# Products that nobody reads, put where TensorE waits, in a two-layer hybrid diffusion step

## What is computed

```python
h = rms_norm(x, norm1_g) * (1 + scale1) + shift1
y = even_mixer(h)      # layer 0: RG-LRU beside differential attention
y = odd_mixer(h)       # layer 1: chunked gated delta rule beside grouped-query attention
x = x + gate1 * y
h = rms_norm(x, norm2_g) * (1 + scale2) + shift2
x = x + gate2 * expert_choice_ffn(h)   # 16 experts, each takes its 80 best tokens
```

## Time and profile before

| what | value |
|---|---|
| median of 3 runs | 1860.54 us (1860.17 to 1864.04) |
| the profiled execution's own time | 1863.33 us |
| its span | 1861.5 us |
| TensorE busy with products and transposes | 1578.3 us, 85% of the span |
| VectorE, ScalarE, GpSimd busy | 647.7, 450.9, 195.5 us |
| mean granted clock of TensorE | 0.922 of full speed |
| DMA | 330.03 MB, mean 177 GB/s |

### The profile page before, as it was taken

The page is one execution under the profiler, slowest core; times in us unless marked ns, Lnnn a source line. Parts: engine busy times, 40 slices in busy tenths (PEclk is TensorE's granted clock), DMA queues, the critical chain, the costliest instruction groups (busy, mean ns, idle before and its releaser), DMA issues.

```text
span 1861.5 us, 37187 instructions
## 1 busy us (share of the span) xinstructions
PE 1578.3 (85%) x16388; PEld 1039.3 (56%) x16388; DVE 647.7 (35%) x1284; ACT 450.9 (24%) x746; POOL 195.5 (11%) x197
## 2 busy tenths in 40 slices
PE   5999965778839999995999977688887957999993
PEld 2554433444517677663555456577775536667762
DVE  5134476552270000004044179734453262000003
ACT  4111284441021111103010055532221031111110
POOL 0000000000001111100000000054640001111103
PEclk8999986998969999997999989788988988999997
DMA  9822370455217999994121100000004225999994
GB/s 342 302 91 90 138 280 6 176 202 205 87 67 274 374 389 383 379 354 136 49 86 49 45 1 1 1 2 3 2 3 159 79 102 175 374 371 391 373 396 153
DMA packets 90316, 330.03 MB, mean 177 GB/s; under 512 B 10709, under 2 KB 16457, under 8 KB 82025
## 3 DMA queue, kind: packets, MB, share of 16 engines
q1 hardware_dynamic: 76016, 287.29, 40.6%
q0 software_dynamic: 9168, 32.65, 6.4%
q10 hardware_dynamic: 5032, 8.65, 1.3%
HBM read 303.79 MB, written 24.78 MB: 177 GB/s over the span
## 4 chain that ended last, share of the span: by engine, by line
PE 72%; DVE 12%; DMA 6%; ACT 5%; issue 5%; POOL 0%; ACTq 0%; DVEq 0%; SPq 0%
PE pairs L192 26%; PE pairs L1245 14%; PE pairs L1257 11%; DMA ring<-in_exp_w 3%; PE pairs L1228 2%; DVE sm L1601 1%; PE pairs L1934 1%; PE pairs L1936 1%; PE pairs L1923 1%; ACT arena L319 1%; PE pairs L961 1%; PE pairs L421 1%; PE pairs L1667 1%; ACT arena L1517 1%; PE pairs L1082 1%
## 5 line engine op out<-in xcount | busy, mean ns | idle before, releaser
L192 PE MATMUL pairs<-hT,ring 128*128 128x128 f32 (+1 forms) x1120 | 305.6, 436 | 2.1 <-ACT hT L319 2.1
L319 ACT ACTIVATE arena<-pairs 128x512 f32<-128x512 f32 (+7 forms) x212 | 129.8, 632 | 501.5 <-PE pairs L192 251.0
L192 PEld LDWEIGHTS pairs<-hT,ring 128*128 128x128 f32 x1120 | 170.2, 192 | 138.3 <-issue 136.8
L192 PE MATMUL pairs<-ring,hT 128*128 128x512 f32 (+1 forms) x448 | 177.4, 557 | 0.0
L1245 PEld LDWEIGHTS pairs<-arena 128*64 128x64 f32 x4096 | 145.5, 139 | 15.1 <-issue 15.0
L1245 PE MATMUL pairs<-arena 128*64 128x80 f32 x4096 | 148.3, 235 | 3.3 <-issue 2.3
L1245 PEld LDWEIGHTS pairs<-arena,ring 128*64 128x64 f32 x4096 | 142.9, 137 | 14.2 <-issue 14.2
L1245 PE MATMUL pairs<-arena,ring 128*64 128x80 f32 x4096 | 145.9, 233 | 0.9 <-issue 0.7
L192 PEld LDWEIGHTS pairs<-ring,hT 128*128 128x128 f32 x448 | 85.0, 190 | 92.0 <-issue 89.0
L1311 DVE TENSOR_SCALAR hT<-pairs,arena 80x512 f32<-80x512 f32 x32 | 23.9, 747 | 274.6 <-ACT hT L1287 274.6
L1257 PE MATMUL pairs<-ring,arena 128*80 128x512 f32 x256 | 112.8, 593 | 1.6 <-DMA ring<-in_exp_w 1.6
(11 more groups left out here) (374 smaller groups left out, 2074.6 us busy)
## 6 DMA issues: line engine op xcount, KB each, us to landing
arena<-in_exp_w SPq DMA_DIRECT2D x48, 2048.0 KB, 19.2
ring<-in_exp_w SPq DMA_DIRECT2D x48, 2048.0 KB, 21.6
ring<-in_w_mod SPq DMA_DIRECT2D x24, 2048.0 KB, 8.0
ring<-in_w_in_ab SPq DMA_DIRECT2D x5, 2048.0 KB, 11.6
ring<-in_w_in_cd SPq DMA_DIRECT2D x5, 2048.0 KB, 8.1
ring<-in_w_out SPq DMA_DIRECT2D x4, 2048.0 KB, 8.0
moe_rows<-arena POOLq DMA_DIRECT2D x2, 2560.0 KB, 15.7
h_rows<-arena POOLq DMA_DIRECT2D x2, 2560.0 KB, 8.4
```

Of the source, the lines that this page charges most:

```text
L192: last = pe.matmul(out, lhs(k), rhs(k), start=(k == 0), stop=(k == KD - 1))
L319: return eng.activation(dst, src, ACT.Copy) if eng is nc.scalar else eng.tensor_copy(dst, src)
```

## The change

A new helper issues n products of the identity with 512 columns of constants, into a PSUM pair or bank that is free at that point; no one reads them, and what is put there next starts its sum anew. The helper is called before the waits named above. In `norm_pe` the pair is also taken ahead of the wait for the squares, and `diff_pe` and `gqa_pe` wait for one unit to be read before the products go to its pair. `spare()` waits for the reader of bank 4's last unit.

```diff
@@ -304,6 +304,11 @@
             pe.wait_ge(S("x_here"), 16 * NT)
             flip_in_pe(pe, "x_in")
 
+        def keep_busy(pe, ps, n):
+
+            for _ in range(n):
+                pe.matmul(ps[:, 0:512], ident, cst[:, 0:4, :].rearrange("p a b -> p (a b)"), start=True, stop=True)
+
         def flip_in_pe(pe, tag):
             for k in range(KD):
                 ps = take(pe, (tag, k))
@@ -479,8 +484,10 @@
 
         def norm_pe(pe, l, n):
             u = ("nrm", l, n)
+            ps = take(pe, u)
+            if n:
+                keep_busy(pe, ps, 2)
             pe.wait_ge(S("sq_add"), ADDS[l, n] + KD - 1)
-            ps = take(pe, u)
             pe.matmul(ps[:, 0:NS], ones, ssum[:, 0:NS], start=True, stop=True)
             finish(pe.matmul(ps[:, NS:T], ones, ssum[:, NS:T], start=True, stop=True), u)
 
@@ -565,6 +572,7 @@
                 ps = take(pe, u)
                 if l == 1 and c == 4 and tp == 0:
 
+                    keep_busy(pe, ps, 6)
                     for k in range(KD):
                         pe.wait_ge(S("h_ready"), 32 * l + 2 * k + 2)
                         for t in range(2):
@@ -946,6 +954,8 @@
                 for t in range(NT):
                     last = pe.transpose(ps[:, t * P:t * P + P], qr[:, t, c], ident)
                 finish(last, u)
+            emptied(pe, ("kT", 2))
+            keep_busy(pe, PSUM[:, units.of["kT", 2][0], :], 3)
             for h in range(4):
                 emptied(pe, ("kT", h))
                 emptied(pe, ("qT", h))
@@ -1258,6 +1269,8 @@
                                              w2[:, f, 512 * half:512 * half + 512], start=(f == 0), stop=(f == FT - 1))
                 last.then_inc(pair_full[3], 1)
 
+            take_at(0, 0, 0)
+            keep_busy(pe, PSUM[:, 0, :], 3)
             gather_T(0, 0)
             beside_first_pe(pe, l)
             base[1:] = units.uses[1:]
@@ -1410,6 +1423,7 @@
         def sum_pe(pe, l):
             un = ("nrm", 1, 0)
             acc = take(pe, un, 3)
+            keep_busy(pe, acc, 12)
             for k in range(KD + 3):
                 if k < KD:
                     if k % 2 == 0:
@@ -1651,6 +1665,8 @@
                 for t in range(NT):
                     last = pe.transpose(ps[:, (t + 1) * P:(t + 2) * P], kdup[:, t, n * P:n * P + P], ident)
                 finish(last, u)
+            emptied(pe, ("gqT", 2))
+            keep_busy(pe, PSUM[:, units.of["gqT", 2][0], :], 3)
             for g in range(4):
                 emptied(pe, ("gqT", g))
             emptied(pe, ("gkT", 0))
@@ -1954,6 +1970,11 @@
                                          vb(j)[r, h, :], start=True, stop=True)
                         if k == 3:
                             b_finish(last, us[h // 2])
+
+            def spare():
+                if banks.uses[4]:
+                    pe.wait_ge(bank_free[4], banks.uses[4])
+                keep_busy(pe, bank_of(4), 1)
 
             def state_a(j):
 
@@ -2000,9 +2021,12 @@
                         if h == 3:
                             b_finish(last, ("st", j, d))
 
+            keep_busy(pe, bank_of(6), 6)
             for m in TILE_ORDER[:2]:
                 kq(m)
+                keep_busy(pe, bank_of(4), 1)
                 kk(m)
+            keep_busy(pe, bank_of(4), 2)
             for j in range(2):
                 am(j)
             for i in range(5):
@@ -2030,13 +2054,17 @@
                     elif s == 5 and i == 2:
                         kk(ST)
                 if i < 4:
-                    for e in range(2):
-                        am(j + 2 + e)
-                for e in range(2):
-                    wu(j + e)
+                    am(j + 2)
+                    spare()
+                    am(j + 3)
+                wu(j)
+                spare()
+                wu(j + 1)
             state_b(8)
             state_a(9)
             state_b(9)
+            pe.wait_ge(bank_free[4], banks.uses[4])
+            keep_busy(pe, bank_of(4), 6)
             pe.wait_ge(S("o_done"), 10)
             for b in range(8):
                 pe.wait_ge(bank_free[b], banks.uses[b])
```

## The result

The changed kernel takes 1834.22 us (median of 4 runs, 1830.64 to 1835.67), the kernel before in the same runs 1862.29 (1860.17 to 1865.01). The ratio is 0.9846, with a 95% interval of 0.9824 to 0.9867: 28 us faster, where 22.5 were forecast. The profiled execution has a span of 1828.7 us and a mean granted clock of 0.954, against 1861.5 and 0.922.

The account below looks back on a forecast made before the run. TensorE was taken to bound the kernel, with gains only from raising its clock behind waits. Terms summed to -24.0 us against 1863.33, giving 1839.3; 1.4 off made 1838 us, range 1828 to 1847 (to 1853 with partial gain and turns).

Parts of the forecast that it names:

- Routers: Norm and router of both layers: products fit the waits, router's low-clock time halves in each layer; -3.2 us.
- first projection: Layer 1's first projection: six products fit a wait of 6.97 us, the 20 passes behind run faster; -2.7 us.
- behind the loop: After the delta rule's loop: six products in a wait of 6.10 us speed the turns behind; -2.1 us.
- Layer 0's experts: Three products in a wait of 5.16 us; turn maybe 0.3 late, first expert faster, whole stage shifts; -2.5 us.
- The sum: Sum between the layers: twelve products end just ahead of the rows; low-clock time behind halves, less later rows; -1.5 us.
- Layer 1's experts: Three products overrun a wait of 1.59 us by 1.0, but the 32 passes behind run faster; -0.9 us.
- Attentions: Differential and grouped-query attention: products overrun their waits by 1.3 and 0.8 us, 1.0 credited back for both; +1.1 us.
- Delta rule: Ahead of the loop: six products in 6.30 us, a bit under half the ceiling of 9; -4 us, ends 0 and 9.
- The ends of rounds: Ends of the delta rule's rounds: spare() holds the clock in short gaps; -8.2 us of 9.7, ends 0 and 9.7.
- the gain reaches the end only in part: Rival, 14%: other engines between TensorE's delta-rule steps limit the gain; about 1849 us.
- Turns hold the clock: Denied by a 3% rival: if turns don't, products ahead of L2053, L1420 and L1877 buy nothing; 1843 us.
- Products that outlast their waits: Slower rival, 6%: clock falls in spite of the products and they outlast their waits; about 1880 us.

Follow-up runs that it names:

- turns: Changed kernel with each product replaced by eight 128x128 transposes; 1834.56 us, ratio 0.9851 to the kernel before.
- Fewer products: Changed kernel without the nine products of the two attentions and of layer 1's experts; 1831.55 us, ratio 0.9833.
- twice as many: Changed kernel with 12 products in place of 6 ahead of both routers and layer 1's first projection; 1842.07 us, ratio 0.9894.
- half as many: Changed kernel without the attentions' and layer 1's experts' products, 3 in place of 6 ahead of both routers and layer 1's first projection; 1837.31 us, ratio 0.9873.
- more fill: Changed kernel with products moved into later attention waits, two more spares in round 3, one product instead of three at layer 1's experts; 1819.93 us, ratio 0.9779.
- The other columns of the table: Distances in two traces: changed kernel with eight transposes for each product (1834.56 us), and with the helper empty (1861.83 us).
- thin spares: Changed kernel with only the nine products of spare() cut to 16 columns; 1845.47 us, ratio 0.9911.
- the second group: Runs of fewer products, twice as many, thin spares and more fill, timed in turn with the kernel before, whose median there was 1862.4 us.

## Why the prediction was right

**The price and the principle.** A product was put at 0.86 us at the high clock; twelve passes took 5.32 with their tail, and six more products cost 3.3 where 5.2 less 1.7 were expected. That the products hold the clock was inferred from other work. It is shown now: the ratio is 0.9995 without them, 0.9967 with 16 columns, 0.9851 with turns, and the nine spares alone lose 11 us when they are cut to 16 columns.

**Routers, first projection, behind the loop.** Forecast -3.2, -2.7 and -2.1, measured -3.2, -2.6 and -1.9. Here the work behind the wait has no gaps, so its time at the low clock could be halved without further thought.

**Layer 0's experts.** Forecast -2.5. The products took 4.76 us, not 5.1, since the clock rose inside them; the turn was not late, and the first expert was over 2.8 us earlier. The stage behind took 1.1 us less in this trace, 0.7 more with turns and 0.4 less without the delta rule's products. No product stands there, so I take it for chance, perhaps of the loads; no run isolates it.

**The sum.** Forecast -1.5, measured -0.8. The row of the step says why, as the prediction had half allowed for: the second quarter of the rows was late.

```profile
845.18 1.31 PE L1434 MATMUL pairs<-cst,arena 128*128 128x128 f32 x10 [0.24 <-DMA arena<-moe_rows]
847.06 1.31 PE L1434 MATMUL pairs<-cst,arena 128*128 128x128 f32 x10 [0.56 <-DMA arena<-moe_rows]
```

At the low clock TensorE had been slow enough never to meet this wait.

**Layer 1's experts.** Forecast -0.9, measured 0: this term was mis-sized. I priced the three products at 0.86 us each, at the high clock. They took 3.34, since the turns ahead of them (L1122) begin behind the long wait for the top-k and run at the low clock, and so did part of the products. Fewer products showed the same time.

**Attentions.** Forecast +1.1, measured -2.0 in this trace and nothing in the medians of the run without them. The overrun is as forecast at the first scores of differential attention (+1.2, for 1.3). What comes back behind them varies by up to 2.7 us from trace to trace, with no product at all. The reason given, that the wait of 3.15 us stays empty, fits: with that wait filled and a product in each later step, the stage gains 5 us on the kernel before, 3.3 of it within the first 16 us.

**Delta rule.** Ahead of the loop the forecast was -4, with ends 0 and 9, and -6.2 came: I took a bit under half the ceiling where two thirds were there. In the changed kernel and eight others with these products the stretch from the first L1877 to the end of round 0's steps takes 34.7 to 34.8 us, all at 1.00, where it took 41.0 at a mean of 0.73, so this is all that the clock had to give there. The ends of rounds were put at -8.2 and brought -9.6, and -12.0 with turns, more than the 9.7 taken for the ceiling, since that left out round 0. Without round 0's 1.6 they brought 8.0 in the changed kernel: round 1's end gave 4.0 where 3.4 was the most expected, round 3's 2.4 of 4.6, round 4's 1.6. So the term came out near its size because what was left out and what was lost about balance.

Round 3's end fell to a mean of 0.73 in this trace, but the empty gap that the prediction named is not enough to bring the clock down. TensorE in order of time ahead of it, and the stretch behind, first the changed kernel:

```profile
1337.65 0.68 PE L1927 MATMUL pairs<-cst,arena 64*64 64x64 f32 x16 [2.34 <-DVE hT L2279]
```

Then the kernel with turns:

```profile
1346.28 0.68 PE L1927 MATMUL pairs<-cst,arena 64*64 64x64 f32 x16 [2.34 <-DVE hT L2279]
1346.30:1355.80 9.50, 8.52 (x146) 1.00 0.02 5
```

The gap is 2.34 us in both, and with turns, with twice as many and with half as many products this end ran at 1.00 and took 9.4 us, where the changed kernel's took 11.8. So it is open what two more spares bring there. With them (more fill) it took 9.4 us too, 2.3 less than in the changed kernel, though the clock fell once ahead of it in that trace, which took 1.5 back.

**The rivals.** That the gain reaches the end only in part was the likeliest of them, and it fell: ahead of the loop a third of the ceiling stayed away though the clock was fully up, but 1834 us is far from its 1849. Turns hold the clock. Products that outlast their waits cost what was said, and but for a part of those at layer 1's experts they ran at the high clock, so no place of the changed kernel lost more than 1.7 us. A penalty under 1% of a typical kernel's span (the Trainium skill, "TensorE: Matmul & The Clock Gate", Part 1) is too small for this kernel: 28 us, 1.5%, came back with the change and 42 us, 2.2%, with the better placed products.

What fell short is the sum: 24.0 forecast, 28.1 measured between the medians, 32.8 between the two spans. Some 5 us of the 32.8 lie where no product was put or none mattered: 1.1 in the rest of layer 0's experts, 1.0 at the decays, 0.6 in the convolution's turns, 2.0 in the attentions. The other columns of the table show the first and the last of these moving in both directions, and the kernel with the delta rule's products alone gained 6.2 us in such places, so I take them for chance. The forecast of 1838 also took 1.4 us off the sum, since the median of three runs lay 2.8 below the profiled execution; the later medians of the kernel before, 1861.3 to 1862.4, lie only 0.9 to 2.0 below it. That the time came within 4 us of the forecast is in part luck: single terms miss by up to 3 us, and they point both ways.

## What to carry to other kernels

Where the engine's clock follows its own work, read each wait together with the clock of the work behind it; half of that work's time at the low level is what can be had, in full where the work has no gaps (in this kernel the routers, the first projection and the turns behind the loop). Fill the wait with work that ends just ahead of the instruction it waits for: in a wait of 6.97 us, 5.2 us of it kept the clock up, 2.6 brought nothing or little at the routers and 1.0 of 2.7 us at the projection, and 10.3 cost 3.3. Where a wait is shorter than the fill, or another empty wait follows it, look for a later place with a free bank before adding anything.

## What the runs showed that I had not expected

- Between an idle stretch and the fall of the clock can lie some work at full speed: with 4.30 us empty the router's first passes took 1.03 us and the second 1.87.
- Near the edge it is chance: the same loop with the same thin spares ran the ends of rounds 0 and 1 at a mean of 1.00 in one kernel and at 0.73 and 0.62 in another, which differ in the products ahead of the loop. Behind the same gap of 2.34 us, and with full spares or turns in it, round 3's end ran at 1.00 in three kernels (turns, twice and half as many) and in part at the low clock in three others (the changed kernel, fewer products, the delta rule's alone). Part of the spread of the kernel before, 1859.8 to 1864.41 us beside the second group, may be this; it wasn't tried.
- 48 transposes hold the clock ahead of the router as well as 12 passes of 512 columns do, and with transposes at every place the time is the same (1834.56 against 1834.22 us).
